# A chunked RWKV-7 recurrence with compact operands, four matmul tiles side by side and two head pairs one subchunk late

## The reference, cut to what matters

```
def step(state, inp):                       # per head: state is 64 x 64, 8 heads, 2048 steps
    r_t, w_t, k_t, v_t, a_t, b_t = inp
    sa = einsum('bhvk,bhk->bhv', state, a_t)
    state = state * w_t[:, :, None, :] + sa[..., None] * b_t[:, :, None, :] + v_t[..., None] * k_t[:, :, None, :]
    y_t = einsum('bhvk,bhk->bhv', state, r_t)
```

## Time and profile before

| | us |
|---|---|
| median of 3 runs | 2329.97 (2316.68, 2329.97, 2513.04) |
| the profiled execution | 2318.93 |
| its span, first to last instruction | 2317.0 |
| TensorE busy | 2225.7 (96%) |
| VectorE busy | 1768.9 (76%) |
| ScalarE busy | 1147.0 (50%) |
| GpSimd busy | 1021.0 (44%) |

### The profile page before, as it was taken

How to read it: one execution, slowest core, us unless ns; L and a number is a source line. 1 busy time by engine, 2 the same in 40 slices (tenths; PEclk the granted TensorE clock), 3 DMA queues, 4 the chain that set the end, 5 groups by cost and what they waited for, 6 DMA issues and landing times.

```text
span 2317.0 us, 42610 instructions
## 1 busy us (share of the span) xinstructions
PE 2225.7 (96%) x16140; PEld 1812.1 (78%) x16140; DVE 1768.9 (76%) x1910; ACT 1147.0 (50%) x1795; POOL 1021.0 (44%) x726
## 2 busy tenths in 40 slices
PE   7999999996989979998999999999999999999998
PEld 5787777775878768887888888788788888887886
DVE  3766798994885466769999998666799999976655
ACT  4656566543545554445444444454554444444543
POOL 4645465571243345536776766100245556541000
PEclk9999999998999989999999999999999999999999
DMA  7374546447566447885434344677643233326774
GB/s 204 91 246 127 196 149 198 136 144 204 160 169 193 129 152 248 270 281 146 163 114 149 111 147 140 220 246 256 229 135 114 91 113 102 102 96 212 246 255 146
DMA packets 435815, 395.54 MB, mean 171 GB/s; under 512 B 59548, under 2 KB 352076, under 8 KB 432332
## 3 DMA queue, kind: packets, MB, share of 16 engines
q1 hardware_dynamic: 407804, 343.06, 47.8%
q10 hardware_dynamic: 27856, 50.34, 6.0%
HBM read 266.97 MB, written 126.35 MB: 170 GB/s over the span
## 4 chain that ended last, share of the span: by engine, by line
PE 54%; DVE 4%; DMA 2%; issue 1%; ACT 1%; SPq 0%; ACTq 0%; POOLq 0%; DVEq 0%; POOL 0%
PE late_bank L133 18%; PE late_bank L134 18%; PE late_bank L135 18%; DVE wt_lo L2862 1%; DMA scratch_a<-p_keep 1%; DVE wt_lo L2908 1%; PE late_bank L2201 1%; DMA o_lo<-scratch_q 0%; ACT wt_hi L2729 0%; DVE p_ub L2871 0%; DMA raw<-in_w_down 0%; DMA raw<-in_w_up 0%; DMA p_keep<-scratch_td 0%; DVE p_ub L2942 0%; DVE p_keep L2942 0%
## 5 line engine op out<-in xcount | busy, mean ns | idle before, releaser
L133 PE MATMUL late_bank<-o_hi,wt_hi 128*128 128x512 f32 x1232 | 481.1, 390 | 9.0 <-DVE p_ub L2929 2.7
L135 PE MATMUL late_bank<-o_hi,wt_lo 128*128 128x512 f32 x1232 | 479.9, 389 | 0.0
L134 PE MATMUL late_bank<-o_lo,wt_hi 128*128 128x512 f32 x1232 | 479.8, 389 | 0.0
L431 POOL TENSOR_TENSOR p_w_lo<-p_w_raw,p_w_hi 128x1024 fp32r<-128x1024 f32 x72 | 188.3, 2616 | 211.7 <-ACT p_w_hi L502 211.7
L133 PEld LDWEIGHTS late_bank<-o_hi,wt_hi 128*128 128x128 f32 x1232 | 231.6, 188 | 60.6 <-issue 8.0
L135 PEld LDWEIGHTS late_bank<-o_hi,wt_lo 128*128 128x128 f32 x1232 | 231.6, 188 | 48.3
L134 PEld LDWEIGHTS late_bank<-o_lo,wt_hi 128*128 128x128 f32 x1232 | 231.7, 188 | 47.8
L2599 POOL TENSOR_TENSOR tsum<-raw 128x512 f32<-128x512 f32 x43 | 105.0, 2442 | 356.1 <-DVE p_ub L2949 177.9
L133 PE MATMUL p_ppr<-p_hT_hi,p_w_hi 128*128 128x512 f32 x576 | 232.8, 404 | 0.2 <-POOL p_w_lo L431 0.2
L133 PE MATMUL late_bank<-wt_hi 128*128 128x512 f32 x572 | 223.1, 390 | 6.0 <-DVE wt_lo L2908 4.7
L135 PE MATMUL p_ppr<-p_hT_hi,p_w_lo 128*128 128x512 f32 x576 | 226.0, 392 | 0.0
(11 more groups left out here) (328 smaller groups left out, 4681.9 us busy)
## 6 DMA issues: line engine op xcount, KB each, us to landing
raw<-in_w_up SPq DMA_DIRECT2D x88, 512.0 KB, 5.1
p_w_raw<-in_w_in SPq DMA_DIRECT2D x72, 512.0 KB, 3.8
scratch_a<-p_keep SPq DMA_DIRECT2D x22, 1280.0 KB, 4.5
raw<-scratch_a SPq DMA_DIRECT2D x96, 256.0 KB, 3.0
raw<-scratch_td SPq DMA_DIRECT2D x52, 256.0 KB, 3.6
p_keep<-scratch_a SPq DMA_DIRECT2D x47, 256.0 KB, 2.9
scratch_a<-p_keep SPq DMA_DIRECT2D x44, 256.0 KB, 2.0
raw<-in_w_down SPq DMA_DIRECT2D x44, 256.0 KB, 4.1
```

The lines of the kernel that those rows point to most:

```text
L133: nc.tensor.matmul(out, lhs_hi, rhs_hi, start=start, stop=False, skip_group_check=again)
L134: nc.tensor.matmul(out, lhs_hi, rhs_lo, start=False, stop=False, skip_group_check=again)
L135: return nc.tensor.matmul(out, lhs_lo, rhs_hi, start=False, stop=stop, skip_group_check=again)
L431: nc.gpsimd.tensor_tensor(w_lo[i][:, :, :], w_raw[i][:, :, :], w_hi[i][:, :, :].bitcast(F32), ALU.subtract).then_inc(s_wl, 1)
```

## The change

It rewrites `phase_recur`, and in phase 1 the copy of v rows (`v_rows`: no longer sorted by head) and the last POOL step (`first_bkc`: two copies in place of a memset and eight copies).

- `bk` becomes `bkc`, [128, 4, 4, 2, 32], with no zeros; masks have one 32-column block; `am`, `ark`, `bkt`, `w` are half as large.
- Products address tiles of 64 or 32 rows and columns, with different heads in different PSUM banks. `bk_transposes` are two groups of 4 instead of four.
- Pairs 2 and 3 run one subchunk behind pairs 0 and 1 (`behind`): a step sigma treats subchunk sigma of pairs 0, 1 and the one before of pairs 2, 3. `read_u` is two ACT instructions, and `advance` adds all pairs and then, at every step, decays the two pairs whose subchunk is odd. Body N has one more `from_state` and `read_u`.
- The adding of -mean to y and its scaling go from DVE to POOL while i < N. The triangular solve is spread over 34 gaps (bodies 0 to 4, and 6 to 10). The mix buffer is doubled, and inverse blocks are loaded two bodies ahead instead of four.

```diff
-        "strict": np.concatenate([(s < t) & (p // C % 2 == h) for h in range(2)], axis=1),
-        "causal": np.concatenate([(s <= t) & (p // C % 2 == h) for h in range(2)], axis=1),
+        "strict": s < t,
+        "causal": s <= t,
...
-                    read_rows(gate, [pm[:, g, :] for g in range(TT)], s_vr)
+                    nc.scalar.activation(gate[:, :, :], pm[:, :, :], ACT.Copy).then_inc(s_vr, 1)
...
-        bk = [scr["first_bk"], scr["bk1"]]
-        w = [scr["w0"], sb("w1", [P, PAIRS, CH, 2 * C])]
+        w = [scr["w0"], sb("w1", [P, 2, DBL, C])]
         am = [scr["am0"], scr["am1"]]
-        ark = [sb(f"ark{i}", [P, UNITS, 2 * C]) for i in range(BATCH)]
-        bkt = [scr["bkt0"], sb("bkt1", [P, UNITS, P])]
-        uv = [sb(f"uv{i}", [P, CH, PAIRS, H]) for i in range(BATCH)]
+        ark = [sb(f"ark{i}", [P, 2 * DBL, C]) for i in range(BATCH)]
+        bkt = [scr["bkt0"], sb("bkt1", [P, DBL, P])]
+        uv = [sb(f"uv{i}", [P, 2, PAIRS, 2, H]) for i in range(BATCH)]
...
+        def behind(i, sigma, jp):
+
+            if jp == 0 or sigma > 0:
+                return i, sigma - jp
+            return i - 1, CH - 1
...
+        GAPS = 8
+        PARTS = 34
...
+                def side_by_side(n, r):
+                    gp.wait_ge(s_in, ONE + n * 32 + 32)
+                    if n > 1:
+                        wait_full(gp, n - 3, f"bk{r}")
+                    js = slice(2 * r, 2 * r + 2)
+                    for m, key in enumerate(("bt", "kt")):
+                        nc.gpsimd.tensor_copy(bkc[n % 2][:, js, :, (n + m) % 2, :], raw[key][:, js, :].rearrange("p j (c t) -> p j c t", t=C)
+                                              ).then_inc(s_bk, 1)
...
+                    if c and i < N:
+                        gp.wait_ge(s_gn, ONE + g + 2)
+                        nc.gpsimd.tensor_tensor(yv, yv, stat[:, 0, :].unsqueeze(2).to_broadcast([P, DBL, H]), ALU.add).then_inc(s_yc, 1)
...
+                    if i + 3 < N:
+                        for r in range(2):
+                            side_by_side(i + 3, r)
+                    if c and i < N:
+                        gp.wait_ge(s_gn, ONE + g + 3)
+                        nc.gpsimd.tensor_tensor(yv, yv, stat[:, 3, :].unsqueeze(2).to_broadcast([P, DBL, H]), ALU.mult).then_inc(s_yc2, 1)
...
+                    def read_u(sigma):
+
+                        k = i * CH + sigma
+                        act.wait_ge(s_p1, ONE + k + 1)
+                        for jp in moving(k):
+                            n, c4 = behind(i, sigma, jp)
+                            c2, at = c4 // 2, quad(c4 % 2, n % 2)
+                            col = (c2 * PAIRS + 2 * jp) * H
+                            nc.scalar.activation(uv[n % BATCH][at, c2, 2 * jp:2 * jp + 2, :, :].rearrange("p j h v -> p h j v"),
+                                                 bank[at, 0:2, col:col + 2 * H].rearrange("p h (j v) -> p h j v", v=H), ACT.Copy).then_inc(s_u[jp], 1)
...
+                        nc.vector.tensor_tensor(new[:, :, :].rearrange("p (b j) v -> p b j v", b=2), banks,
+                                                old[:, :, :].rearrange("p (b j) v -> p b j v", b=2), ALU.add).then_inc(s_sum, 1)
+                        jp = 1 - sigma % 2
+                        n, c4 = behind(i, sigma, jp)
+                        at, js = n * 2 + c4 // 2, slice(2 * jp, 2 * jp + 2)
+                        dve.wait_ge(s_sum, ONE + k)
+                        nc.vector.tensor_tensor(new[:, js, :], new[:, js, :], scr["pend"][:, js, at:at + 1].to_broadcast([P, 2, H]), ALU.mult
+                                                ).then_inc(s_sn, 1)
...
-                        nc.vector.tensor_tensor(dst[:, :, :].rearrange("p u (h t) -> p u h t", t=C),
-                                                g2[:, :, at:at + C].unsqueeze(2).to_broadcast([P, UNITS, 2, C]),
-                                                mask[:, :, :].unsqueeze(1).to_broadcast([P, UNITS, 2, C]), ALU.mult).then_inc(done, 1)
+                        nc.vector.tensor_tensor(dst[:, :, :], g2[:, :, at:at + C], mask[:, :].unsqueeze(1).to_broadcast([P, 2 * DBL, C]), ALU.mult
...
+                    def from_state(sigma):
+                        k = i * CH + sigma
+                        pe.wait_ge(s_sn, ONE + k)
+                        for j2 in range(2):
+                            for jp in moving(k):
+                                n, c4 = behind(i, sigma, jp)
+                                e, c2, j = c4 % 2, c4 // 2, 2 * jp + j2
+                                at = (c2 * PAIRS + j) * H
+                                for h in range(2):
+                                    last = nc.tensor.matmul(bank[quad(e, n % 2), h, at:at + H], w[n % 2][half(h), e, 2 * j + c2, :],
+                                                            state(k)[half(h), j, :], start=False, stop=True, skip_group_check=True)
                         last.then_inc(s_p1, 1)
...
+                    def to_state(sigma):
+                        k = i * CH + sigma
+                        pe.wait_ge(s_u[0], ONE + k + 1)
+                        pe.wait_ge(s_u[1], ONE + k)
+                        for j2 in range(2):
+                            for jp in moving(k):
+                                n, c4 = behind(i, sigma, jp)
+                                e, c2, j = c4 % 2, c4 // 2, 2 * jp + j2
+                                for h in range(2):
+                                    last = nc.tensor.matmul(bank[half(h), UPDATE[jp], j2 * H:(j2 + 1) * H], bkt[n % 2][rows(e), 2 * j + c2, half(h)],
+                                                            uv[n % BATCH][rows(e), c2, j, h, :], start=True, stop=True)
...
+                                    c4 = 2 * c2 + e
+                                    for h in range(2):
+                                        last = nc.tensor.matmul(bank[rows(e), GB + h, at:at + 2 * C], bkc[p][half(h), j, c4, :, :].rearrange("p k t -> p (k t)"),
+                                                                far[half(h), :, j, c4 * C:c4 * C + C], start=True, stop=True)
...
                     if b:
                         wait_read(pe, i - 1, "w1")
+                    if b or i == N:
                         from_state(0)
+                    if b:
+                        wait_read(pe, i - 1, "bk1")
+                    if o:
+                        from_r(0)
+                    if b:
+                        to_state(0)
+                    if a1:
+                        grams(range(0, 2))
+                    if d:
+                        y_transposes(range(0, 2 if i == N else PAIRS))
+                    if b:
+                        from_state(1)
+                    if o:
+                        from_uv()
+                    if b:
+                        to_state(1)
+                    if a1:
+                        grams(range(2, PAIRS))
                     if a2:
                         bk_transposes(0)
-                    if b:
-                        to_state(0)
-                    if o:
-                        from_r(0)
-                    if d:
-                        pe.wait_ge(s_yc2, ONE + i - 2)
-                        turn("y", lambda o, j: nc.tensor.transpose(o[:, j * SC:(j + 1) * SC], y[q][:, 2 * j:2 * j + 2, :].rearrange("p h v -> p (h v)"),
-                                                                   ident[:, :]), PAIRS)
-                    if b:
-                        from_state(1)
-                    if a2:
-                        bk_transposes(1)
-                    if b:
-                        to_state(1)
-                    if o:
-                        from_uv()
-                    if a2:
-                        bk_transposes(2)
+                    if i == N:
+                        y_transposes(range(2, PAIRS))
                     if b:
                         from_state(2)
-                    if a2:
-                        bk_transposes(3)
+                    if o:
+                        from_r(1)
                     if b:
                         to_state(2)
-                    if o:
-                        from_r(1)
                     if a2:
                         z0_products()
                     if b:
                         from_state(3)
-                    if a1:
-                        grams(0)
+                    if a2:
+                        w_products()
                     if b:
                         to_state(3)
+                    if o and a2:
+                        pe.wait_ge(s_yr, ONE + i)
                     if a2:
-                        w_products()
-                    if a1:
-                        for j in range(1, PAIRS):
-                            grams(j)
-                    if a2:
+                        bk_transposes(1)
                         wait_read(pe, i, "z0")
                         z()
```

(57 more changed lines are left out.)

348 lines of the change are left out of this document (141 added, 207 removed).

## The result

| | us |
|---|---|
| changed kernel, median | 2352.8 |
| kernel before, on the same chip | 2326.9 |
| ratio of the two | 1.0117, 95% interval 1.0093 to 1.0142 |
| forecast, with its range | 2270, 2243 to 2298 |
| profiled execution of the changed kernel: time, span | 2348.77, 2347.0 |

One disturbed run of each kernel (7573 and 2513 us) stands in the medians and is left out of the ratio. The slowdown is clear of the noise, though under 2%. The span grew by 30.0 us: 6.7 up to the second iteration (`from_state` of iteration 0 at 559.37 for 558.46, iteration 0 23.69 us for 17.94), 20.8 in the fifteen iterations that the prediction summed (266.6 for 245.8), 2.5 behind them.

What follows compares the result with a forecast made beforehand. The prediction took VectorE to bound iterations with the triangular solve and TensorE the others. From 2318.93 us it took 46.7 for fifteen iterations and 3 at the start, added 1 at the end: 2270 us, range 2243 to 2298.

Steps and rivals of the forecast that it cites:

- The price of a pass on four tiles: Recurrence on TensorE: a pass on four tiles costs 14 ns, against 29 on two, plus 0.13 us per group.
- TensorE's sum: One recurrence iteration after the change: TensorE's groups add up to 11.0 us, 4.4 less than before.
- the chain: Iterations without solve: dependent steps from from_state through to_state to the decay, with TensorE's filler, become the bound, 12.1 us.
- TensorE's time was taken as passes times their price: Recurrence: each new TensorE group costed as its passes at 14 ns plus 0.13 us, e.g. 16 passes 0.35 us.
- That rival: Recurrence: TensorE waits in every step, so its clock falls to 1.2 GHz; about 2335 us, chance 4%.
- Solve iterations at 14.8: The six recurrence iterations holding most of the triangular solve, VectorE-bound before, were to take 14.8 us each.
- The stretching beside GpSimd: Solve iterations: VectorE instructions with two SBUF inputs stand still during GpSimd's passes, +1.9 us; adds reading PSUM never stretch.
- The start, -3 with bounds of 0 and -5: Start of the recurrence: inverse loaded earlier, but chunk 2's first Grams behind the first from_state; -3 us.
- DMA hidden: Recurrence loads: 10.6 us of DMA time fits into a 12.1 us iteration, with little to spare.
- four signs that it would be wrong: Recurrence trace: free iterations above 13.3 us, passes at 29 ns, clock under 0.95, first iteration waiting longer for b and k.

Runs made afterwards that it cites:

- yzw_long: Changed kernel with the short passes of y, z0 and w replaced in their places by a few long ones of the same duration; 2300.0 us, ratio 0.9911.
- y_long: Changed kernel with y's 128 short passes replaced in their places by three long products of the same TensorE time, 244 instructions less an iteration; 2327.8 us, ratio 1.0018.
- fewer_y: Changed kernel with y almost left out: from_r and from_uv keep one product each of 16 and 32; 2340.0 us, ratio 1.0062.
- yzw_short: As yzw_long, but the long products of y and z0 are cut to 4 columns, same number of instructions; 2320.4 us, ratio 0.9987.
- no_solve: Changed kernel with each step of the triangular solve cut to one element; 2350.0 us, ratio 1.0122.
- start: Changed kernel with b, k, a and r of the third chunk requested ahead of the last twelve block loads of the start; 2348.7 us, ratio 1.0114.
- light_dma: Changed kernel without most loads of the stage from the fifth chunk of 128 tokens on, stores kept; 2331.8 us, ratio 1.0049.

## Why the prediction was wrong

- **The price of a pass on four tiles** (14 ns, a group 0.13 more) was right: 16 passes 0.35 us, 64 passes 1.03. So were TensorE's sum (11.0; 11.6 in yzw_long) and **the chain** (12.1; 12.6 in the undisturbed iterations of yzw_long, 12.95 in the fit). The step from `from_state` to `to_state` took 1.42 for 1.38, the other 1.42 for 1.38.
- **The step that failed: TensorE's time was taken as passes times their price.** It has a second bound, its instructions. The change adds 88 passes, that is 176 instructions, to some 870, and at the same time makes each pass half as long, so 4.1 blocks of 256 come due in 12.1 us, 2.9 us each, where a block that is waited for takes 4.6. The prediction counted the passes of each new group (8 to 16, 32 to 64) for their nanoseconds alone. Price by the fit: 2.4 us an iteration, 34 us in 14. The Trainium skill, "Runtime: NRT & Kernel Launch", section "Instruction fetch mechanics", tells of blocks of 256 instructions, refilled in 16 KiB, and calls the crossing of a border mostly hidden. The trace agrees on the size of the block and its packet; it disagrees on hidden, with some 44 us of stops. The same section gives TensorE room for 2048 instructions; a packet that starts 2.0 us after TensorE entered the block just ahead does not look like seven blocks in hand. The kernel before already had the sign of it, mid-group `issue` stops of up to 1.5 us, which were read over (timeline of TensorE before):

```profile
690.86 0.45 PE L1719 MATMUL late_bank<-ar,bk 128*64 128x64 f32 x8
692.81 1.79 PE L1719 MATMUL late_bank<-ar,bk 128*64 128x64 f32 x40 [1.50 <-issue]
```

- **The second step that failed: the sum had no term for the clock. That rival was put at 4%, and it happened.** Its argument against itself, that a half-speed TensorE is never idle and gets the clock back, held only in part (at 1.2 GHz TensorE was busy 96 of 109 us) and was no protection: the clock came back 13 times and fell 13 times, at 1.2 GHz for 0.43 of the time, just over the four tenths from which that rival decides. Price by the fit: 2.7 us an iteration, 38 us in 14. Its own figure of 2335 was some 15 us short; it had no term for the stops.
- The two are not independent. y_long against fewer_y (1.0018 and 1.0062) and yzw_long against yzw_short (0.9911 and 0.9987) show that less work lowers the clock, the second pair with hardly any stops; y_long against the changed kernel, with TensorE's time kept and 244 instructions less, shows the time at 1.2 GHz falling from 7.8 to 2.4 us (in its second fastest execution, and with another kind of pass). How the 5.1 us divide is the fit's word, borne out by five other runs to within 0.7 us an iteration.
- **Solve iterations at 14.8** can't be seen in the changed kernel (no_solve changes nothing), but in yzw_long they take 14.2 to 15.0 at the full clock, with VectorE busy 13.2 to 13.5 (15 forecast). The stretching beside GpSimd is there, on solve steps and decays and never on the add from PSUM, as the earlier trace rows had it (each decay of over 0.8 us and each of these solve steps of over 0.7 us ran beside a two-input pass of GpSimd):

```profile
L1483 DVE TENSOR_TENSOR p_inv<-p_inv,p_prod x60: 208/404/1311, 561.8 to 752.4; 128x30 f32<-128x30 f32 x4, 128x58 f32<-128x58 f32 x4, 128x84 f32<-128x84 f32 x4, 128x108 f32<-128x108 f32 x4
```

```profile
L1529 DVE TENSOR_TENSOR p_st<-p_st,chunk_decay x63: 291/292/1329, 571.7 to 849.3; 128x128 f32<-128x128 f32 x63
```

```profile
L1523 DVE TENSOR_TENSOR p_st<-late_bank,p_st x63: 424/425/427, 571.2 to 848.8; 128x256 f32<-128x256 f32 x63
```

- **The start, -3 with bounds of 0 and -5**, was +6.7. The mechanism was named (the Grams of chunk 2, the third, behind `from_state`, b and k requested late), and then not allowed to cost anything. The Grams started late (timeline of the changed kernel, below). The bracket names no semaphore, but in the `start` run, which only moves their loads ahead, they start at 561.50 after 0.71 us of idle time:

```profile
567.72 1.13 PE L1723 MATMUL late_bank<-p_ar,first_bkc 64*64 64x64 f32 x32 [6.50 <-issue]
```

- *DMA hidden*: not wholly (light_dma, -16 us).
- **The account**: forecast for the 14 full iterations 13.3 us in the mean (6x14.8 + 8x12.1, by 14), measured 18.03: -0.3 in the base, +2.4 stops, +2.7 clock. Times 14 that is 66.9 us; with 9.7 more than forecast at the start, 0.6 in the last iteration and 1.5 behind it, it makes, to within 0.1, the 78.6 us between 2270.2 and 2348.77. Of the prediction's four signs that it would be wrong, the long free iterations, the clock below 0.95 (0.78) and the first iteration came true; the passes at 29 ns did not.

## What to carry to other kernels

Count an engine's instructions as well as its time: here a block of 256 TensorE instructions that had to be waited for took 4.6 us, so where every block is waited for, a float32 product of two passes, four instructions, comes to an estimated 70 ns (4.6 us by 64) however small its tile. A rewrite that removes zeros by cutting products smaller adds instructions, and it pays only as far as its program can follow. And an engine that is made faster than the chain around it can lose its clock: look in the trace before for stops in the middle of a group and for clock falls, and price both along with the passes.

## What the runs showed of the hardware that was not expected

- TensorE's program arrives in 16 KB packets of 256 instructions, one at a time: where TensorE waits for one, it starts 1.1 to 3.2 us after the border ahead, moves in about 1.1 us, and TensorE goes on 1.40 us later. Over all blocks, the packet starts 1.3 us after the border in the quarter of the blocks with the least DMA traffic at the border and 1.9 to 2.2 in the two quarters with the most.
- Less work can be slower: yzw_short does an estimated 2.7 us less an iteration than yzw_long at full clock and takes 18 us longer in all, at a granted clock of 0.72 for 0.94.
- Filler that lifts the clock (0.78 to 0.96 and 0.90) cost 20 and 16 us: here the raised clock didn't pay for the filler, which stood on the path.
- Still open: how data packets hold the program's packets back, what share of the clock's falls the stops cause, and why the `start` run gave its 6.5 us back.
